# Two transformer blocks on one Trainium2 core: the last two units of each stage and the norms behind them run by halves of the tokens

## The reference

```
h = rms_norm(x) * gain (+ shift in block 1)
y = mixing(h)            # projections, attention and other branches, then h' @ w_out
x = x + gain * rms_norm(y)
h = rms_norm(x) * gain (+ shift in block 1)
y = conv_ffn(h)          # h @ w_up, causal convolution, gelu * value, then @ w_down
x = x + gain * rms_norm(y)
```

## Time and profile before

| | us |
|---|---|
| median of 3 runs (1769.74 to 1774.49) | 1773.53 |
| the profiled execution, its own time | 1771.58 |
| its span | 1769.8 |
| PE busy | 1577.1 (89%) |
| PE weight loads busy | 1234.1 (70%) |
| DVE / ACT / POOL busy | 653.6 / 670.2 / 655.1 |

### The profile page before, as it was taken

How to read it: one execution, slowest core, us unless ns; L and a number is a source line. 1 busy time by engine, 2 the same in 40 slices (tenths; PEclk the granted TensorE clock), 3 DMA queues, 4 the chain that set the end, 5 groups by cost and what they waited for, 6 DMA issues and landing times.

```text
span 1769.8 us, 18968 instructions
## 1 busy us (share of the span) xinstructions
PE 1577.1 (89%) x7336; PEld 1234.1 (70%) x7336; DVE 653.6 (37%) x939; ACT 670.2 (38%) x996; POOL 655.1 (37%) x300
## 2 busy tenths in 40 slices
PE   5879766689999999789988898999986999999995
PEld 2679643368888888558875567777873788888874
DVE  3655364344444400234014432144314555555002
ACT  3332452344444422232224345353323555554221
POOL 1283200434444444434421125334433444445442
PEclk9889886799999999889999899999998999999998
DMA  7454201512222233302411123222221122222321
GB/s 325 178 225 157 84 1 24 125 54 89 89 91 93 72 100 96 110 25 95 143 48 36 36 72 110 81 67 82 90 95 48 48 95 95 95 95 71 98 93 48
DMA packets 27141, 162.73 MB, mean 92 GB/s; under 512 B 3240, under 2 KB 3368, under 8 KB 12360
## 3 DMA queue, kind: packets, MB, share of 16 engines
q1 hardware_dynamic: 23616, 151.01, 24.8%
q10 hardware_dynamic: 3464, 10.88, 2.5%
HBM read 157.15 MB, written 4.72 MB: 91 GB/s over the span
## 4 chain that ended last, share of the span: by engine, by line
PE 82%; DVE 8%; ACT 3%; POOL 2%; DMA 2%; issue 1%; POOLq 0%; DVEq 0%; ACTq 0%; SPq 0%
PE ps L1431 71%; PE ps L1418 4%; PE ps L1634 1%; DMA raw<-w_up_dram 1%; PE ps L1648 1%; DVE S L1359 1%; PE ps L1661 1%; POOL WL L626 1%; PE ps L1425 1%; PE ps L1390 1%; ACT S L821 1%; DMA xT<-x_dram 1%; DVE nt L1099 1%; PE ps L1578 1%; DVE S L1346 1%
## 5 line engine op out<-in xcount | busy, mean ns | idle before, releaser
L626 POOL TENSOR_TENSOR WL<-raw,WH 128x1024 fp32r<-128x1024 f32 (+3 forms) x184 | 366.8, 2008 | 719.1 <-ACT WH L731 718.3
L1431 PE MATMUL ps<-hH,WH 128*128 128x512 f32 x1136 | 462.2, 407 | 21.4 <-DVE hL L1115 16.4
L1431 PE MATMUL ps<-hL,WH 128*128 128x512 f32 x1136 | 454.2, 400 | 0.0
L1431 PE MATMUL ps<-hH,WL 128*128 128x512 f32 x1136 | 453.6, 399 | 0.0
L659 POOL TENSOR_TENSOR WL<-raw,WH 128x2048 fp32r<-128x2048 f32 x44 | 208.4, 4737 | 288.0 <-ACT WH L853 288.0
L1431 PEld LDWEIGHTS ps<-hH,WH 128*128 128x128 f32 x1136 | 217.2, 191 | 79.5 <-issue 20.8
L1431 PEld LDWEIGHTS ps<-hH,WL 128*128 128x128 f32 x1136 | 216.7, 191 | 53.9
L1431 PEld LDWEIGHTS ps<-hL,WH 128*128 128x128 f32 x1136 | 217.2, 191 | 51.1 <-issue 0.5
L731 ACT ACTIVATE WH<-raw 128x1024 fp32r<-128x1024 f32 (+3 forms) x184 | 160.1, 896 | 242.2 <-PE ps L1431 231.5
L1431 PE MATMUL ps<-hidH,WH 128*128 128x512 f32 x352 | 139.5, 396 | 0.0
L1431 PE MATMUL ps<-hidH,WL 128*128 128x512 f32 x352 | 137.1, 389 | 0.0
(11 more groups left out here) (228 smaller groups left out, 2258.3 us busy)
## 6 DMA issues: line engine op xcount, KB each, us to landing
raw<-w_up_dram SPq DMA_DIRECT2D x44, 1024.0 KB, 4.8
raw<-w_in_dram SPq DMA_DIRECT2D x36, 1024.0 KB, 4.9
adaw<-w_ada_dram SPq DMA_DIRECT2D x20, 1024.0 KB, 6.7
raw<-w_down_dram SPq DMA_DIRECT2D x16, 768.0 KB, 4.2
raw<-w_down_dram SPq DMA_DIRECT2D x16, 640.0 KB, 3.9
xT<-x_dram ACTq DMA_DIRECT2D x2, 2048.0 KB, 11.1
adap<-w_ada_dram SPq DMA_DIRECT2D x4, 1024.0 KB, 20.6
raw<-w_mem_kv_dram SPq DMA_DIRECT2D x4, 1024.0 KB, 4.8
```

The source lines that it names most:

```text
L626: pool.tensor_tensor(WL[:, d % 2, 0:nk, cols], raw[:, d % 2, 0:nk, cols], WH[:, d % 2, 0:nk, cols].bitcast(F32), ALU.subtract).then_inc(lo ...
L1431: mm = pe.matmul(out, lhs[x], rhs[y], start=(first and i == 0), stop=(last and i == 2))
```

## The change

Tokens 0 to 255 are half 0, tokens 256 to 511 half 1. For the last two units u, v of each of the four stages, and for the norms behind them, every instruction is issued twice, once for each half, 256 tokens wide. The sums of squares go to bank 5 (half 0) or 7 (half 1), the spread roots to bank 4 or 6, and each half has its own semaphores. The first two units of the next stage (`head`) run by halves too and are issued half 0 of both first. The `up` loop of PE starts at its second pair. The last four units of the two w_down products keep the halves in different banks. The last stage has no next one: its residual and the output transfers run by halves. The step list behind a stage becomes `boundary`:

```diff
+LOW = 2
+HS = S // 2
+SUM_BANK, RSTD_BANK = (5, 7), (4, 6)
+TAILS = {N_POST1: (D_OUT + 2, D_OUT + 3), N_POSTF1: (D_IN2 - 2, D_IN2 - 1),
+         N_POST2: (D_OUT2 + 2, D_OUT2 + 3), N_POSTF2: (D_END - 2, D_END - 1)}
+TAIL_UNITS = [d for pair in TAILS.values() for d in pair]
+BY_HALF = TAIL_UNITS + [d - 2 for d in (D_IN2 - 2, D_IN2 - 1, D_END - 2, D_END - 1)]
...
-        def with_squares(d0, d1, per, n):
+        def both(n, c):
+            return [("squares", n, k, half) for k in (c, c + 1) for half in (0, 1)]
+        def with_squares(d0, n):
+            u, v = TAILS[n]
+            per = 1 if n in (N_POST1, N_POST2) else 4
             out, late = [], []
-            for d in range(d0, d1):
+            for d in range(d0, u):
                 out += [("seg", d, 0), ("seg", d, 1)] + late
                 late = []
                 if (d - d0) % per == per - 1:
-                    c = 2 * ((d - d0) // per)
                     out += [("evac_y", d)]
-                    late = [("squares", n, c), ("squares", n, c + 1)]
-                    if d == d1 - 1:
-                        out, late = out + late, []
-                if d + 2 < D_END:
-                    out += [("split", d + 2)]
+                    late = both(n, 2 * ((d - d0) // per))
+                out += [("split", d + 2)]
...
             return out + late
-        def residual(n, nxt, between=()):
-            return [("norm", n), ("resid", n), *between] + [("squares", nxt, k) for k in range(KD)] + [("norm", nxt), ("apply", nxt)]
+        def boundary(n, nxt=None):
+            u, v = TAILS[n]
+            first = 4 if n in (N_POST1, N_POST2) else 6
+            ends = (u, v) if first == 4 else (v,)
+            out = [("tail", u, 0), ("tail", v, 0)] + [("evac_half", d, 0) for d in ends]
+            out += [("tail", u, 1)] + [("squares", n, k, 0) for k in range(first, KD)]
+            out += [("split", u + 2)] if nxt else []
+            out += [("norm", n, 0), ("tail", v, 1, 0), ("spread", n, 0), ("tail", v, 1, 1)]
+            out += [("evac_half", d, 1) for d in ends] + [("squares", n, k, 1) for k in range(first, KD)]
+            out += [("split", v + 2)] if nxt else []
+            out += [("resid", n, 0)]
+            if nxt is None:
+                return out + [("norm", n, 1), ("spread", n, 1), ("resid", n, 1)]
+            out += [("squares", nxt, k, 0) for k in range(KD // 2)] + [("norm", n, 1)]
+            out += [("squares", nxt, k, 0) for k in range(KD // 2, KD)] + [("spread", n, 1), ("norm", nxt, 0), ("spread", nxt, 0)]
+            out += [("apply", nxt, 0), ("head", nxt, 0, 0), ("resid", n, 1), ("head", nxt, 1, 0)]
+            out += [("squares", nxt, k, 1) for k in range(KD)] + [("norm", nxt, 1), ("spread", nxt, 1)]
+            return out + [("apply", nxt, 1), ("head", nxt, 0, 1), ("head", nxt, 1, 1)]
...
+            def evac_half(d, half):
+                y, c = y_of(d)
+                sc.wait_ge(pe_seg, tail_end(d, half))
+                src = ps[:, 2 * pair_of(d) + half, :].rearrange("p (m n) -> p m n", m=2)
+                sc.activation(y[:, c:c + 2, HS * half:HS * half + HS], src, ACT.Copy).then_inc(
+                    banks_read[pair_of(d)] if half else y_half, 1)
...
+            def half_products(d, half, m, q):
+                src, nk = source_of(d), unit_source(d)[1]
+                k0 = DOWN_K0[q] if nk in DOWN_K else 0
+                cols, toks = slice(m * P, (m + 1) * P), slice(half * HS, half * HS + HS)
+                for k in range(nk):
+                    mm = product(ps[:, 2 * pair_of(d) + half, m * HS:(m + 1) * HS], (WH[:, d % 2, k, cols], WL[:, d % 2, k, cols]),
+                                 (src[0][:, k0 + k, toks], src[1][:, k0 + k, toks]),
+                                 m == 0 and k == 0 and q == 0, m == 1 and k == nk - 1 and (q == 3 or nk not in DOWN_K))
+                return mm
+            def tail(d, half, m_only=None):
...
+                if half == 0:
+                    pe.wait_ge(lo_done, LOW * (d + 1))
...
+                for m in (0, 1) if m_only is None else (m_only,):
+                    mm = half_products(d, half, m, q)
+                if m_only != 0:
+                    mm.then_inc(pe_seg, 1)
+            def head(n, i, half):
+                d0 = {N_PREF1: D_UP1, N_PRE2: D_IN2, N_PREF2: D_UP2}[n]
+                d, toks = d0 + i, slice(half * HS, half * HS + HS)
+                if half == 0:
+                    pe.wait_ge(lo_done, LOW * (d + 1))
+                    pe.wait_ge(banks_read[pair_of(d)], bank_use(d))
+                for k in range(KD):
+                    wait_h(pe, n, k, half)
+                    for m in range(2):
...
+                        if half == 1 and k == KD - 1:
+                            mm.then_inc(pe_seg, 1)
...
-                with pe.Fori(0, FF_PAIRS) as j:
+                with pe.Fori(1, FF_PAIRS) as j:
```

More of the change, by code:

```diff
@@ L389, in pairs_before @@
             return sum(1 for t in TILES23[:n] if t[0] == "mem" or t[2] % 2 == 1)
-        steps = [("start",)] + [("squares", N_PRE1, k) for k in range(KD)]
-        steps += [("ada_row", 0), ("ada", 0), ("ada_turn", 0), ("row_turn", 0), ("norm", N_PRE1), ("split", 0)]
-        steps += [("ada_end", 0), ("apply", N_PRE1, 0, 4), ("seg", D_IN, 0, 0, 4)]
+        steps = [("start",)] + [("squares", N_PRE1, k, 0) for k in range(KD)]
+        steps += [("ada_row", 0), ("ada", 0), ("ada_turn", 0), ("row_turn", 0), ("norm", N_PRE1, 0), ("spread", N_PRE1, 0), ("split", 0)]
+        steps += [("ada_end", 0), ("apply", N_PRE1, 0, 0, 4), ("seg", D_IN, 0, 0, 4)]
         steps += [("ada_row", 1), ("ada", 1), ("ada_turn", 1), ("row_turn", 1)]
-        steps += [("ada_end", 1), ("apply", N_PRE1, 4, KD), ("split", 1), ("trig",)]
+        steps += [("ada_end", 1), ("apply", N_PRE1, 0, 4, KD), ("split", 1), ("trig",)]
         e = r = 0
@@ L493, in build @@
         steps += [("mem_load",)] + sum(beside, []) + sum(turned_beside, [])
-        steps += [("squares", N_MEM, k) for k in range(KD)] + [("norm", N_MEM), ("apply", N_MEM)]
+        steps += [("squares", N_MEM, k, 0) for k in range(KD)] + [("norm", N_MEM, 0), ("spread", N_MEM, 0), ("apply", N_MEM, 0)]
         for d in range(D_KV, D_BR1):
@@ L759, in apply @@
+            def apply(n, half, k0=0, k1=KD):
+                cols = norm_cols(n, half)
                 dst = memH if n == N_MEM else hH
                 for k in range(k0, k1):
[L761 to L762 removed]
+                    t = dl[:, k % 4, cols]
+                    sc.wait_ge(scaled[half], KD * SPLITS[half][n] + k + 1)
                     if n in shifts:
[L764 to L765 removed]
@@ L983, in merge @@
                 sc.activation(mgH[:, c, :], merged[:, c, :], ACT.Copy).then_inc(m_hi, 1)
-            walk({"start": start, "row_turn": row_turn, "trig": trig_tables, "split": split, "squares": squares, "norm": norm, "apply": apply,
+            walk({"start": start, "row_turn": row_turn, "trig": trig_tables, "evac_half": evac_half, "split": split, "squares": squares, "norm": norm, "apply": apply,
                   "spread_hi": spread_hi_tile, "spread_lo": spread_lo_tiles, "evac_in": evac_in, "turn": turn,
@@ L1479, in seg @@
                 s = d % 2
-                if not by_token(d):
+                if d in BY_HALF:
+                    for half in (0, 1):
+                        mm = half_products(d, half, m, q)
+                elif not by_token(d):
                     w = MEM if D_KV <= d < D_KV + 4 else S
@@ L1662, in back2 @@
                 mm.then_inc(pv2_done, 1)
-            walk({"ada_row": ada_row, "row_turn": row_turn, "ada_turn": ada_turn, "squares": squares, "norm": norm, "seg": seg, "turn": turn, "pool": pool_step, "front": front,
+            walk({"ada_row": ada_row, "row_turn": row_turn, "ada_turn": ada_turn, "squares": squares, "spread": spread, "tail": tail, "head": head, "seg": seg, "turn": turn, "pool": pool_step, "front": front,
                   "mid": mid, "back": back, "combine": combine, "up": up, "bias_rows": bias_rows, "front2": front2,
```

270 lines of the change are left out of this document (153 added, 117 removed).

## The result

The changed kernel took 1803.6 us (median of 4 runs, 1802.2 to 1809.1), against 1774.0 for the kernel before in the same series: ratio 1.018, 95% interval 1.016 to 1.020. The forecast had slower, and the reasons for it, but only half of the loss: 1788, with 1802 as the upper end of the range.

What follows compares the result with a forecast made beforehand. PE was taken to bound most of the span, the four holes (7%) being all to win; 5.7 + 10.8 + 5.1 - 6.0 = +15.6 on 1771.6 gave 1787.2, taken as 1788, range 1770 to 1802.

Steps and rivals of the forecast that it cites:

- (b): First hole: POOL's cut of v+2 stands ahead of half 0's six residual additions, which start at 26.8 instead of 18.3.
- (a): First hole: rounding and cut of u+2 stand ahead of half 0's norm; PE waits 3.7 us for the spread.
- (e): Between the next stage's heads: half 1's squares stand behind both half 0 heads, leaving a second hole of 8.6 us.
- the late squares behind w_out_2: Behind w_out_2: squares of chunks 2 and 3 now stand directly ahead of u, costing 3.5 us.
- their cover by a transfer behind w_out: Behind w_out: the 21.54 us transfer of unit u+2's weights lands after the late squares, so they cost nothing.
- the wait for weights in both loops: `up` loops: next gate weights take 9.3 us, only 5.7 of value unit covers them, so PE waits 3.6.
- The end, 29.7 from u: Last stage by halves: 29.7 us from u to the end instead of 36.5; -6.0 with 0.8 for two units ahead.
- The wait for the first spread, 3.7: Behind w_down: PE waits 3.7 us for half 0's spread, then finishes the rest of v at 19.4.
- the tail is slow too: Rival: clock falls in the first spread's wait, so v's rest and squares run at half rate; 1796 to 1800, chance 0.11.
- Behind w_out, +5.1 from the landing on: Behind w_out, from the landing of u+2's weights: 66.9 us instead of 61.8, +5.1.
- the forecast's 0.9: Holes: the same walk through the kernel before gave a hole 0.9 us shorter than read, so 0.9 was added.
- The clock rival: Rival: with tails and heads laid into the holes PE stays at 2.4 GHz, 5.4 us less a hole; 1772, chance 0.12.

Runs made afterwards that it cites:

- the second profile: The changed kernel run and profiled once more, unchanged: 1804.7 us, ratio 1.0185.
- the kernel with the weights first: Kernel with three orders, plus ACT's rounding of the next gate weights ahead of the gate's two seeds in the `up` loops: 1753.7 us, ratio 0.988.
- the kernel with three orders: Changed kernel with additions ahead of v+2's cut, u+2's cut behind half 0's norm, half 1's squares between the heads: 1755.0 us, ratio 0.990.
- the filled holes: Kernel with the weights first, plus small products of ones where PE would wait for the norms, at three boundaries: 1749.8 us, ratio 0.987.
- the kernel with the squares between the heads: Changed kernel with half 1's squares of the new x between the chunks of half 0's second head in PE's program: 1788.2 us, ratio 1.010.

## Why the forecast was half right

**The direction and the mechanisms held.** The cut ahead of the additions (b), the cut and the rounding ahead of the norm (a), the second hole (e), the late squares behind w_out_2 (3.5 forecast, 3.8 read), their cover by a transfer behind w_out, and the wait for weights in both loops (3.6 forecast; 3.5 and 3.7 read) are all in the trace, and an experiment bears on each. The points named as refutation did not occur: behind w_down the first head came 41.1 us after u (33 would have been the limit), and the second hole was 9.2.

**The size failed.** 1803.6 lies above the range's end of 1802. The four stretches came out 17.7 us above the forecast's sum in the first profile, 15.1 in the second. In the first these are 8.0 behind w_out, 1.8 behind w_down, 4.8 behind w_out_2 and 3.1 at the end. The terms of the sum that were mis-sized:

- *"PE waits 3.6" in the loop, and no more.* The wait was right (3.5 and 3.7), but the forecast let PE go on at full rate behind it. The clock had fallen (0.50 in 400.64 to 403.60), and the second pair lost 2.5 us behind w_out and 1.65 behind w_out_2: 4.2 us which the forecast had at nothing (3.3 in the second profile). In the kernel with the weights first, with a wait of 2.5, the clock stayed at 1.00 and the second pair took 22.5, where the kernel with three orders has 24.1.
- *The end, 29.7 from u.* It took 32.9. From the last product to the last addition the forecast had 10.6 (16.0 to 26.6), and it took 13.1 (1790.92 to 1804.04). DVE's two additions of each half take 0.95 beside POOL's, 0.43 alone. That is 1.0 us in half 1; in half 0 it holds up DVE's norm of half 1 by 1.1 us; and that spread ran cold (1.22 instead of 0.71).

```profile
1797.77 1.26 DVE L1200 SCALAR_TENSOR_TENSOR dl<-yff,vec,ps 128x256 f32<-128x256 f32 x3 [1.32 <-PE ps L1506]
1799.06 0.94 DVE L1206 TENSOR_TENSOR xT<-xT,dl 128x256 f32<-128x256 f32 x1
1801.22 0.95 DVE L1206 TENSOR_TENSOR xT<-xT,dl 128x256 f32<-128x256 f32 x1
```

- *The wait for the first spread, 3.7, "rest of v: 19.4".* The wait was read at 3.6 behind w_down and 3.9 behind w_out_2, but what stands behind it is dearer: behind w_down the clock had fallen in it, so the rest of v took 2.9 instead of 1.8 and the squares of the new x 7.0 at a mean clock of 0.57. When the wait was taken away, 4.9 to 7.2 came back at each boundary, not 3.9. This was the rival "the tail is slow too", 1796 to 1800, that had 0.11: as a mechanism it was right, and it came on top of the sum.
- *Behind w_out, +5.1 from the landing on.* The weights landed 3.4 later in the profile (the split starts at 328.92, not 325.51): 2.6 of that is the execution's, and 0.8 the stage's. From there to the second gate unit it took 71.7, not 66.9. ACT has the rounding ahead of the root, so spread, rest of v and squares all start from the landing, PE cold. The forecast had this order right and the way from the landing 4.8 too short.

```profile
328.92 2.00 ACT L792 ACTIVATE WH<-raw 128x1024 fp32r<-128x1024 f32 x2 [3.12 <-issue]
330.83 0.19 ACT L820 ACTIVATE nt<-nt 128x2 f32<-128x2 f32 x1
```

(The view names no releaser for these 3.12 us. The load was issued at 307.40; as long as the 21.54 in the earlier trace rows it lands at 328.9, so I take the transfer for it.)

What most of these have in common: a loss of clock was entered only at the two heads of a boundary (2.3 and 1.8). The changed kernel has up to four waits of PE there, and slow products behind most. Of the 17.7 us, the 4.2 in the second pairs is this, by the granted clock and the length of the unit; the 3.1 of the end is DVE's additions, the cold spread and hand-overs, read in the trace. Of the other 10.4 the trace shows the place: with the forecast's 0.9 put to the first hole, its steps have the first head at 39.7 behind w_down, 48.8 behind w_out_2 (81.6 less the 33.7 from there to the end of the walk) and 28.1 from the landing behind w_out, and it came at 41.1, 52.0 and 30.6. So 1.4, 3.2 and 2.5, 7.1 together, were lost ahead of the first heads. How much of that is cold products and how much hand-overs was not taken apart and stays open.

**The clock rival** ("the clock holds", 1772) was wrong: 0.50 in the first 3 us of the first heads (780.60 to 783.60) and 0.95 to 1.00 in the second holes, with 0.50 behind them. The Trainium skill (TensorE: Matmul & The Clock Gate, Part 1) has activity release the clock; the filled holes agree behind w_down (1.00 against 0.50) and not at the second gate unit behind w_out (0.50, against 1.00 without fillers).

**A reading that was off.** The forecast reads PE as busy for half of each of the first three holes or less; the earlier trace rows give 0.47, 0.52 and 0.52. Nothing in the sum rests on it.

**Left open:** why a second gate unit starts at full clock in one execution and at half clock in another after the same wait; and whether the few us in untouched stretches have a part that is the change's.

## What to carry to other kernels

Cutting a serial tail in two pays only if each engine's program is reordered with it: what was hidden behind the whole (a weight cut, squares for the next norm) stands in front of something urgent once the halves interleave. Here the same halves cost 30 us in one order and gained 19 in another (20 to 24 with the weights first and the fillers). List, for every engine, what stands ahead of the first instruction that the new chain needs; and price a wait of PE as the wait plus the slow products that may follow it, once for each wait and not once for each boundary.

## What the runs showed of the hardware

- DVE's TENSOR_SCALAR, and its instructions with two inputs in SBUF, end with the POOL cut that they meet, however small they are: 2 columns took 1.84 us (1.04 with 4 columns in another kernel), two 128 x 128 scalings 3.55 as TENSOR_SCALAR and 3.67 with two SBUF inputs. Not every DVE instruction on SBUF waits: beside the same cut the sum over 256 columns (L1167) kept its 0.42 and the reciprocal its 0.17. With one input in PSUM the same engine kept 0.42 to 0.48. POOL and DVE of the changed kernel behind w_down:

```profile
751.68 4.67 POOL L686 TENSOR_TENSOR WL<-raw,WH 128x1024 fp32r<-128x1024 f32 x2 [9.64 <-ACT WH L792]
751.79 0.42 DVE L1167 TENSOR_REDUCE nt<-nt 128x2 f32<-128x256 f32 x1
752.24 1.84 DVE L1168 TENSOR_SCALAR nt<-nt 128x2 f32<-128x2 f32 x1
754.35 0.17 DVE L1171 RECIPROCAL nt<-nt 128x2 f32<-128x2 f32 x1 [0.27 <-ACT nt L820]
754.55 2.08 DVE L1173 TENSOR_SCALAR nt<-ident_t,nt 128x128 f32<-128x128 f32 x2
```

- Half-width additions: POOL 0.73 each against 1.24 for the full width, DVE 0.43 alone. Where the two overlap, the later one waits: DVE's took 0.95 when POOL's had started first (1799.06 behind 1799.01), and POOL's 0.93 when DVE's had (1386.40 behind 1386.32).
- The clock may fall at the first products of a new stage, not in the wait: in the kernel with three orders it was 1.00 over the whole first hole and 0.50 over the first 3 us of the head.

```profile
1338.26:1352.98 14.72, 8.73 (x36) 5.36 (x37) 10.60 (x24) 8.39 (x22) 10.33 (x10) 1.00 0.42 143
1352.98:1356.00 3.02, 3.02 (x16) 3.02 (x15) 3.02 (x9) 1.76 (x5) 2.16 (x3) 0.50 0.00 0
```

- It does not fall behind every wait. PE waited 3.5 to 3.7 us ahead of the second gate unit sixteen times in eight profiles; the clock over the next 3 us was 0.50 to 0.72 in fifteen, and 1.00 in one, after 3.7 us, in the kernel with the squares between the heads. Behind ten waits of 2.5 to 2.7 us in five profiles it was 1.00 in seven and 0.50 to 0.55 in three. The one:

```profile
1412.68:1415.68 3.00, 3.00 (x13) 2.45 (x14) 2.73 (x4) 0.79 (x1) 2.07 (x1) 1.00 0.66 186
```

- Stretches with the same program differ between profiled executions by up to 9 us over some 1380, so a step of 2 or 3 us is better read in its own stretch of the trace than in the total.
